# Attention steps dealt out anew in two blocks of a one-core transformer kernel, with pre-scaled queries

## The reference, cut to what matters

```python
s = jnp.einsum('bqhcd,bkhcd->bhcqk', qi, kf) * scale     # scale = 64 ** -0.5
s = jnp.where(kpos[None, :] <= qpos[:, None], s, NEG)
p = jax.nn.softmax(s, axis=-1)
w = p[:, :, 0] - lam * p[:, :, 1]                          # layer A only
```

## Time and profile before

| | us |
|---|---|
| median of three runs (lowest, highest) | 978.34 (976.88, 978.77) |
| the profiled execution | 978.28 |
| its span, first to last instruction | 976.6 |
| TensorE busy, share of the span | 938.0, 96% |
| TensorE's weight loads | 790.2, 81% |
| VectorE busy | 587.7, 60% |
| ScalarE busy | 476.0, 49% |
| GpSimd busy | 70.8, 7% |
| mean granted TensorE clock | 0.990 |

### The profile page before, as it was taken

The page is one execution under the profiler, slowest core; times in us unless marked ns, Lnnn a source line. Parts: engine busy times, 40 slices in busy tenths (PEclk is TensorE's granted clock), DMA queues, the critical chain, the costliest instruction groups (busy, mean ns, idle before and its releaser), DMA issues.

```text
span 976.6 us, 13275 instructions
## 1 busy us (share of the span) xinstructions
PE 938.0 (96%) x4758; PEld 790.2 (81%) x4758; DVE 587.7 (60%) x801; ACT 476.0 (49%) x699; POOL 70.8 (7%) x132
## 2 busy tenths in 40 slices
PE   5999989999999999999999999999897999999998
PEld 4788778888888887778888888888776888888887
DVE  3777766756565576543856555558887374545543
ACT  4765565544444365562744444446335364344341
POOL 2101030100000010001100000002133000000000
PEclk9999999999999999899999999999898999999999
DMA  8844223765655443221765565555332055555551
GB/s 278 298 143 132 87 92 131 258 209 174 201 185 191 154 172 130 87 87 45 258 217 193 176 207 178 167 181 191 113 108 85 3 178 199 182 181 198 179 172 43
DMA packets 95435, 157.77 MB, mean 162 GB/s; under 512 B 5928, under 2 KB 37624, under 8 KB 95392
## 3 DMA queue, kind: packets, MB, share of 16 engines
q1 hardware_dynamic: 93872, 155.09, 47.7%
q10 hardware_dynamic: 1488, 2.10, 0.7%
q0 software_dynamic: 32, 0.02, 0.0%
HBM read 156.12 MB, written 1.06 MB: 161 GB/s over the span
## 4 chain that ended last, share of the span: by engine, by line
PE 85%; DVE 6%; ACT 4%; POOL 2%; issue 2%; DMA 1%; SPq 0%; ACTq 0%; DVEq 0%; POOLq 0%
PE proj L1405 8%; PE proj L1407 8%; PE proj L1406 8%; PE turn L1445 5%; PE score L1405 5%; PE proj L1445 5%; PE score L1406 5%; PE score L1407 5%; PE outp L1405 5%; PE outp L1407 5%; PE outp L1406 5%; PE proj L1449 3%; PE turn L1449 3%; PE turn L1432 2%; PE score L1569 2%
## 5 line engine op out<-in xcount | busy, mean ns | idle before, releaser
L1693 DVE TENSOR_TENSOR wlo<-raw,whi 128x2048 fp32r<-128x2048 f32 x145 | 329.7, 2278 | 221.5 <-ACT whi L1194 147.6
L1194 ACT ACTIVATE whi<-raw 128x2048 fp32r<-128x2048 f32 x64 | 122.6, 1916 | 170.0 <-PE outp L1407 57.5
L1405 PE MATMUL proj<-whi,set 128*128 128x512 f32 (+1 forms) x432 | 174.7, 404 | 9.8 <-DVE wlo L1693 7.0
L1188 ACT ACTIVATE whi<-raw 128x2048 fp32r<-128x2048 f32 (+1 forms) x81 | 153.0, 1901 | 47.6 <-PE outp L1407 18.4
L1407 PE MATMUL proj<-whi,set 128*128 128x512 f32 (+1 forms) x432 | 169.5, 392 | 0.0
L1406 PE MATMUL proj<-wlo,set 128*128 128x512 f32 (+1 forms) x432 | 169.2, 392 | 0.0
L1405 PEld LDWEIGHTS proj<-whi,set 128*128 128x128 f32 x432 | 83.0, 192 | 27.1 <-issue 9.2
L1407 PEld LDWEIGHTS proj<-whi,set 128*128 128x128 f32 x432 | 82.6, 191 | 17.6
L1406 PEld LDWEIGHTS proj<-wlo,set 128*128 128x128 f32 x432 | 83.1, 192 | 15.6
L1405 PE MATMUL score<-whi,set 128*128 128x512 f32 x236 | 92.8, 393 | 0.4 <-ACT e L1331 0.4
L1405 PE MATMUL outp<-whi,set 128*128 128x512 f32 x236 | 92.8, 393 | 0.4 <-issue 0.4
(11 more groups left out here) (207 smaller groups left out, 1240.0 us busy)
## 6 DMA issues: line engine op xcount, KB each, us to landing
raw<-in_a_w_up SPq DMA_DIRECT2D x32, 512.0 KB, 4.3
raw<-in_a_w_down SPq DMA_DIRECT2D x32, 512.0 KB, 4.5
raw<-in_b_w_up SPq DMA_DIRECT2D x32, 512.0 KB, 4.2
raw<-in_b_w_down SPq DMA_DIRECT2D x32, 512.0 KB, 4.4
raw<-in_w_gate SPq DMA_DIRECT2D x22, 512.0 KB, 4.0
raw<-in_w_up SPq DMA_DIRECT2D x22, 512.0 KB, 4.9
raw<-in_w_down SPq DMA_DIRECT2D x22, 512.0 KB, 3.9
raw<-in_a_w_in SPq DMA_DIRECT2D x20, 512.0 KB, 6.6
```

The costliest lines, as they stand in the source:

```text
L1188: act.activation(shaped(whi, u), shaped(raw, u), ACT.Copy).then_inc(hi_done, 1)
L1194: act.activation(shaped(whi, u), shaped(raw, u), ACT.Copy).then_inc(hi_done, 1)
L1405: pe.matmul(out_, hi, wh, start=start, stop=False)
L1693: dve.tensor_tensor(shaped(wlo, u), shaped(raw, u), shaped(whi, u), ALU.subtract).then_inc(lo_done, 1)
```

## The change

- `heads(...)` takes a scale, and ScalarE's copy L1309 applies it, so that the queries in `qk` are already multiplied by 64 ** -0.5. L1869 is gone: the maximum L1868 is written negated, and the exp has no scale. The fill of `flip`, which carried the inverse of the scale to the bias, is 1.
- The step `scores` is split: `scores` keeps TensorE's part, a new step `exps` has the maximum and the exps. By default `exps` follows at once; `diff_pair` writes the scores of both items first and then their `exps`.
- Layer A: the unit order is `qk0`, `v0`, `vm`, ... instead of `qk0`, `vm`, `v0`. The heads of `qk0` are transposed right behind the first half of `v0`, the first diff pair goes before the second half, and all later items, `turn_heads`, `norm`, `rope_chunk` and `split` steps take new places between the product tiles.
- `finish_attention` in layer A has `mix` of the last pair behind `turn_operand`.
- Layer B: the memory and causal items, the `turn_heads`, the evacuation of `kv1` and the `split` steps take new places.

The core of the diff (lines of no consequence left out):

```diff
+        def exps(*items):
+            for it in items:
+                st = add("exps")
+                st.it = it
...
-        mB.append(half_around(lambda: turn_mem("b_mem_norm", 1, 2 * memA[1] + 2), vm, 0, 0, x1[0]))
+        mB.append(half_around(lambda: turn_mem("b_mem_norm", 1, 2 * memA[1] + 2), v0, 0, 0, x1[0]))
+        h_use = [turn_heads(zq[:, 1], [0, 1, 2, 3], qk_pieces(0), rope_ready(r0.rope))[-1]]
+        d = diff_pair(0)
+        exps(*d[0:2])
+        multiply(v0[1], 0, UK, x1[1], "P", False, True, hold=True)
+        mix(d[0]); mix(d[1])
+        ev = evacuate(v0[1], [((0, 512), lambda t: v[:, t, 0:512])], rs_x)
+        split(v0[1] + AHEAD)
+        turn_weights(d[0]); turn_weights(d[1])
+        d += diff_pair(1)
+        exps(*d[2:4])
+        mul_chunk_half(vm, 0, 0, x1, mixed=d[2:4])
+        attend(d[0], vneed); attend(d[1], vneed); turn_weights(d[2]); turn_weights(d[3])
+        norm(d[0:2])
         mul_chunk_half(vm, 1, 0, x1)
...
+        attend(d[2], vneed); attend(d[3], vneed)
+        norm(d[2:4])
+        multiply(qk1[0], 0, 0, x1[0], "P", True, False, hold=True, tiles=[0])
+        qm_use = turn_heads(zq[:, 0], [0, 1], heads(0, 6, 2, SCALE), chunk_ready(ev.chunk))[-1]
+        multiply(qk1[0], 0, 0, x1[0], "P", True, False, hold=True, tiles=[1])
+        split(qk1[0] + AHEAD)
+        m = mem_pair(0)
         mul_chunk_half(qk1, 1, 0, x1, mixed=m[0:2])
         r1 = rope_chunk(qk1[1], 1, rope1, rs_x, zfree[1])
+        turn_weights(m[0]); turn_weights(m[1])
+        m += mem_pair(1)
         mul_chunk_half(qk2, 0, 0, x1, mixed=m[2:4])
...
+        mul_mem(0, 0)
         mul_mem(0, 1)
         mix(d[6]); mix(d[7])
         split(memB[0] + AHEAD)
+        attend(d[4], vneed); attend(d[5], vneed)
         norm(d[4:6])
+        h_use.append(turn_heads(zq[:, 0], [0, 1, 2, 3], qk_pieces(4), rope_ready(r2.rope))[-1])
         mul_mem(1, 0)
+        turn_weights(d[6]); turn_weights(d[7])
+        d += diff_pair(4)
+        exps(*d[8:10])
+        attend(d[6], vneed); o8 = attend(d[7], vneed)
+        norm(d[6:8])
+        mul_mem(1, 1)
         mix(d[8]); mix(d[9])
         split(memB[1] + AHEAD)
+        turn_weights(d[8]); turn_weights(d[9])
+        d += diff_pair(5)
+        exps(*d[10:12])
         ev = evacuate(memB[1], mem_pieces(1), rs_mem, slot_free=zfree[1])
...
             o1 = turn_operand(o_nat, 0, [(None, oset, 0)], (o_evac, o_half), 2 * last_qset_unit + 2)[-1]
+            if items[0].kind == "diff":
+                mix(items[2]); mix(items[3])
             attend(items[0], vneed); attend(items[1], vneed)
...
+        multiply(kv1[1], 0, UK, xk[1], "P", False, True, hold=True, tiles=[1])
         c = [causal_item(0, 0), causal_item(0, 1)]
-        mul_chunk_half(kv1, 1, 0, xk, mixed=(c[0], c[1]))
         ev = evacuate(kv1[1], ...)
...
+        multiply(v1[1], 0, UK, xk[1], "P", False, True, hold=True, tiles=[1])
+        mix(c[4]); mix(c[5])
         ev = evacuate(v1[1], [((0, 512), lambda t: v[:, t, 256:768])], rs_b)
+        split(v1[1] + AHEAD)
         attend(c[2], v_first); attend(c[3], v_first); turn_weights(c[4]); turn_weights(c[5])
...
-                    behind(dve.tensor_reduce(it.nm, S, AX_X, ALU.max))
-                    dve.tensor_scalar(it.nm, it.nm, -SCALE, None, ALU.mult)\
-                       .then_inc(nmax_done, 1)
+                    dve.tensor_reduce(it.nm, S, AX_X, ALU.max, negate=True).then_inc(nmax_done, 1)
```

More of the change, by code:

```diff
@@ L391, in build, with scores @@
         ITEMS = []
-        def scores(kind, pair, t, q, k, need):
+        def scores(kind, pair, t, q, k, need, later=False):
             it = Step()
@@ L409, in scores @@
             st.it = it
-            return it
+            if not later:
+                exps(it)
+            return it
+        def exps(*items):
+            for it in items:
+                st = add("exps")
+                st.it = it
         def mix(it):
@@ L528, in build @@
                       rs_x, slot_free=zfree[0])
-        def mem_item(p, t, qneed, kneed):
-            return scores("mem", p, t, 6 + p, mk[:, p, :], max(qneed, kneed))
-        def diff_item(h, t):
-            return scores("diff", h, t, h, qk[:, 16 + h, :], h_use[h // 2])
-        h_use = [turn_heads(zq[:, 1], [0, 1, 2, 3], qk_pieces(0), rope_ready(r0.rope))[-1]]
-        zfree[1] = h_use[0] + 1
-        multiply(v0[0], 0, 0, x1[0], "P", True, False, hold=True, tiles=[0])
-        d = [diff_item(0, 0), diff_item(0, 1)]
@@ L540, in build @@
-        qm_use = turn_heads(zq[:, 0], [0, 1], heads(0, 6, 2), chunk_ready(ev.chunk))[-1]
-        zfree[0] = qm_use + 1
-        multiply(v0[0], 0, 0, x1[0], "P", True, False, hold=True, tiles=[1])
-        mix(d[0]); mix(d[1])
-        split(v0[0] + AHEAD)
-        turn_weights(d[0]); turn_weights(d[1])
-        d += [diff_item(1, 0), diff_item(1, 1)]
-        multiply(v0[1], 0, UK, x1[1], "P", False, True, hold=True)
-        mix(d[2]); mix(d[3])
-        ev = evacuate(v0[1], [((0, 512), lambda t: v[:, t, 0:512])], rs_x)
@@ L569, in build @@
+        turn_weights(m[2]); turn_weights(m[3])
+        d += diff_pair(2)
+        exps(*d[4:6])
+        multiply(qk2[1], 0, UK, x1[1], "P", False, True, hold=True, tiles=[1])
+        mix(d[4]); mix(d[5])
+        r2 = rope_chunk(qk2[1], 0, rope1, rs_x, zfree[0])
+        split(qk2[1] + AHEAD)
         memB = chunk_units(A["b_w_mem_kv"][0], [(0, 512)])
@@ L572, in mul_mem @@
             multiply(memB[h], 1, UK * h, mB[h], "P", h == 0, h == 1, hold=True, tiles=[t])
+        attend(m[2], memV); attend(m[3], memV)
+        turn_weights(d[4]); turn_weights(d[5])
+        d += diff_pair(3)
+        exps(*d[6:8])
         mul_mem(0, 0)
-        mix(d[4]); mix(d[5])
-        h_use.append(turn_heads(zq[:, 0], [0, 1, 2, 3], qk_pieces(4), rope_ready(r2.rope))[-1])
-        zfree[0] = h_use[2] + 1
-        turn_weights(d[4]); turn_weights(d[5])
-        d += [diff_item(3, 0), diff_item(3, 1)]
         mul_mem(0, 1)
@@ L889, in build @@
         tile(gb, 1, 0, xb)
[L890 removed]
+        qa_use = turn_heads(zq[:, 0], [0, 1, 2, 3], heads(0, 0, 4, SCALE), lambda t: (qn_done, t + 1))[-1]
         zfree[0] = qa_use + 1
@@ L1320, in _ @@
                     act.wait_ge(heads_zeroed, 2)
-                elif st.kind == "scores":
+                elif st.kind == "exps":
                     it = st.it
```

80 lines of the change are left out of this document (40 added, 40 removed).

## The result

The changed kernel takes 992.21 us (median of four runs, 990.99 to 992.61) against 977.61 (976.54 to 978.77) for the kernel before on the same chip: a ratio of 1.0141, 95% interval 1.0129 to 1.0153. The table is of one profiled execution of each.

What follows compares the result with a forecast made beforehand. TensorE, nearly never idle, was taken as the bound, so new waits and clock decide: span 976.6 + 12 (layer A waits) + 6.2 (clock) - 1.7 (layer B) - 0.7 (last layer) = 992.4, plus 1.7: 994.1 us, range 981 to 1001.

Steps and rivals of the forecast that it cites:

- Place A: Layer A, first `turn_heads` and the scores behind it: TensorE waits for T banks and six copies, 3.9 us.
- Place B: Layer A, `qk2[0]`: TensorE waits for bank P from the rope of `qk1[1]`, 1.4 us.
- Place C: Layer A, weights of the fifth pair (d8, d9): mix behind `norm(d[6:8])`, waits 3.4 and 1.2, 4.6 us.
- Place D: Layer A, weights of the last pair: mix behind `turn_operand` and memB's evacuation, waits 5.2 and 1.1, 6.3 us.
- The small ones: Layer A: second item of d6, d7 waits 0.8 for a T bank, two more of 0.15; 1.1 us.
- The clock: Layer A: granted clock falls to half behind A, C and D, costing 2.6, 1.1 and 2.5; +6.2 us.
- GpSimd beside VectorE: Layer A norms: a split's subtraction lengthens GpSimd's first operation; only the norm of d4, d5 meets one, 2 us.
- Layer B: Layer B's stage: waits 6.2 against 6.4, clock 1.8 against 3.3; together -1.7 us, bounds -7 and +3.
- L1869: Removed small operation, 40 times 0.18 us: 0.7 us less in the last layer, elsewhere counted inside the chains.
- The clock stays up: Rival 1: the waits come but the clock does not fall; 991 at most, 986 with the lower bound; chance 0.24.
- Half of it: Rival 2: place C or D is covered, a step put in front being already done; 980 to 984; chance 0.12.
- Faster: the holes of before are what counts: Rival 3: layer B, 379 to 401 us, gives back 4.05 + 3.3, layer A 4.8; 968 or 973; chance 0.08.

Runs made afterwards that it cites:

- fill: Changed kernel plus 13 useless matmuls in layer A, 7 ahead of the first `turn_heads` and 6 between it and the scores: 988.63 us.
- half of v0 ahead: Changed kernel with the first tile of v0's second half moved ahead of the first `turn_heads` in layer A: 986.69 us.
- shift: Changed kernel plus 7 useless matmuls (1.6 us) between the two tiles of v0's second half, so all that follows comes later: 992.49 us.
- mix ahead: Changed kernel with the mix of layer A's last pair (d10, d11) right behind its exps, ahead of memB's evacuation and `turn_operand`: 985.18 us.
- arithmetic alone: Kernel before plus only pre-scaled queries, negated maxima, no L1869, exps without a scale; both layers in the old order: 975.64 us.
- layer B's order: Kernel before plus the new arithmetic and layer B's new order, layer A in the old order: 974.07 us.
- four mends: Changed kernel, layer A: v0 tile ahead of `turn_heads`, norm(d6, d7) behind mix(d8, d9), memB's evacuation and mix(d10, d11) earlier: 982.50 us.
- tiles back: Changed kernel with layer A reordered, a product tile behind the scores of every pair, two at the front and three at the end: 985.17 us.

## Why the prediction was right

The forecast was 994 and the slowdown in layer A; both came. In the span it was +12 of waits and +6.2 of clock in layer A, -1.7 in layer B and -0.7 in the last layer; measured were +8.8, +8.1, -1.0 and -0.8, and -1.1 ahead of the first stage, which belongs to none of its steps. By its steps:

**Place A**, forecast 1.9 + 0.3 + 1.7 = 3.9, measured 1.83 + 0.15 + 1.56 = 3.5: right in each part, and with the releasers named. **Place B**, 1.4 and 1.40.

**Place C**, forecast 3.4 + 1.2, measured 2.99 + 0.70. GpSimd's chain took 2.06 us, from 132.44 to 134.50 (forecast 2.3). The second part was mis-sized: a mix behind another takes 1.2 us, but TensorE is itself busy for 0.5 of them with the first item's weights.

**Place D**, forecast 5.2 + 1.1, measured 3.79 + 0.71: the term furthest off. I counted TensorE's own work between scores and weights as 1.6 us; it took 2.5, from 141.15 to 143.65, as the clock was still down from place C when it began:

```profile
141.15 1.83 PE L1469 MATMUL turn<-ident,o_nat 128*128 128x128 f32 x8
```

At full clock this group takes 1.04 to 1.09. In the three kernels whose slow stretch behind place C was only 3.4 us long (fill, half of v0 ahead, shift) the same wait is 4.53 or 4.54, here in the kernel with the fill:

```profile
144.54 0.33 PE L1633 MATMUL turn<-ident,e 128*128 128x128 f32 x1 [4.53 <-DVE e L1927]
```

So a slow stretch ahead of a wait shortens the wait, and costs less than half of its length. The other 0.5 us is the chain, 6.3 us for 6.8: the split that I put in VectorE's way (0.3) had ended at 139.5, before the scores of d11 had, at 141.4. The experiment with the mix ahead confirms the chain, since with the mix moved bank T was what was late.

**The small ones**, forecast 1.1, measured 0.4. The sum of the waits in layer A was then 13.6 and not 17.3, which is +8.8 over before and not +12.

**The clock**, forecast +6.2 in layer A. All three falls came, and the stage is 16.9 longer where 18.2 were forecast. Of these 16.9, 8.8 are waits; the other 8.1 are busy time of the same matmuls, which is clock. The rows agree nearly: in the three slow stretches TensorE is busy 6.34 + 5.82 + 4.86 = 17.0 us, and half of that is 8.5. So that term was some 2 us short and the waits 3.2 long: two errors of opposite sign, and that the total is nearer than its parts is luck. By falls, half of the busy time is 3.2 for A, 2.9 for C and 2.4 for D, where I had 2.6, 1.1 and 2.5. The mis-sized one is C: I had most of its slow stretch lie in D's wait, but it ended at 142.7 and that wait began at 143.65, so TensorE had work in nearly all of it.

**GpSimd beside VectorE.** The norm of d4, d5 did meet a split: DVE's L1730 and POOL's L1141 in the first two rows of this timeline. The norm of d6, d7 in the last two met none; it is the one that held DVE.

```profile
124.69 2.29 DVE L1730 TENSOR_TENSOR wlo<-raw,whi 128x2048 fp32r<-128x2048 f32 x1 [0.46 <-ACT whi L1225]
...
125.45 1.57 POOL L1141 TENSOR_SCALAR newton<-stat 128x2 f32<-128x2 f32 x1 [42.45 <-ACT junk L1377]
...
132.44 0.19 POOL L1141 TENSOR_SCALAR newton<-stat 128x2 f32<-128x2 f32 x1 [3.54 <-ACT junk L1377]
...
134.53 0.61 DVE L1931 SCALAR_TENSOR_TENSOR o_nat<-outp,stat,subln 128x128 f32<-128x128 f32 x2 [4.06 <-POOL stat L1146]
```

1.57 against 0.19, and the long one ends at 127.02, within 0.04 us of the split's end. The Trainium skill, "SBUF — State Buffer", section "SBUF: two separate sides", says that a VectorE operation with two SBUF inputs and a GpSimd operation that reads SBUF shut each other out for the whole of the one that started first. The trace agrees: the split had started first, and the GpSimd operation ended 0.04 us behind it.

**Layer B**, forecast -1.7 (waits 6.2 for 6.4, clock 1.8 for 3.3), measured -1.0: waits 6.1 for 6.3, and 6.8 us of slow stretch on both sides, in one piece before and in two after. The 2.66 before L1442 was forecast as 2.6. The waits were right in sum, though 0.8 us of what left this stage's old waits came from the arithmetic (6.3 to 5.5) and the order itself added 0.6. The clock's part was a coin: 98.68 or 101.82 us for the same order in two kernels.

**L1869**, forecast -0.7 for the last layer and nothing elsewhere but inside the chains. The last layer gave -0.8 (-0.5 in the kernel with the arithmetic alone, whose medians give -2.4 in all). It was mis-sized in the two attention stages (0.4 and 1.1), where I had it inside the chains and gave it no sum of its own.

**The rivals.** "The clock stays up" is out by the windows. Its 991 has 1.5 us in it that no step gives, and less 4 it is 987, not 986. "Half of it" is out by places C and D. "Faster: the holes of before are what counts" was right in its place and wrong in its size: with the arithmetic, layer B's order and one more step moved, the same stage gives 7.0 us, 4.0 of them clock; it could not cover layer A. The Trainium skill, "VectorE: DVE Perf Modes", section "Rules for kernel authors", advises to minimise the count of operations in a chain. The trace agrees in sign only: of the 8 us that 40 operations of 0.2 us would be, at most 2.4 came.

## What to carry to other kernels

Walk each wait from the end of the last thing that feeds it, step by step through the lists of all engines, and count TensorE's own work in between at the clock that it has there: that gave every wait of the changed kernel to within 1.5 us, its releaser included. It did not carry over to orders with several steps moved at once: four mends had 9.3 us of waits for the expected 4.4, tiles back 12.7 for 2.9. When product tiles are dealt out between attention steps, look at what is left behind the last scores, and at whether a split stands ahead of a mix, an evacuation or a norm on VectorE and ScalarE. Mend one wait at a time and look where it goes: place C's reappeared at D, while the one in layer B, with tiles behind it, was gained in full. That these are the two things that decide is my reading of these orders; the kernel with tiles back shows that the first alone does not.

## What the runs showed of the hardware

- The granted clock falls to half, for 3.4 us, 6.8 and once 10.2, behind some idle stretches of TensorE and not behind others of the same length. At place A it was regular: 6.8 us at half behind holes of 3.5 us in five kernels, 3.4 us behind one of 1.9 us in two, none without a hole in three. In layer B it was not: the same instructions with the same waits had 6.8 us of slow clock in the kernel after, 3.4 in the shifted one and none with the mix ahead. In the table the slow length goes from 10.7 to 44.3 us, worth some 10 us of time by the fitted 0.3.
- It also differs between executions of one kernel: the one with layer B's order took 972.8 us at a mean clock of 0.995 and 977.0 at 0.987, the program being the same. A change that is worth 2 us can be hidden by that, so the waits of one profile tell more than two medians.
- A slow stretch ahead of a wait shortens it: place D's was 3.79 us with 6.8 us at half clock ahead of it and 4.53 with 3.4.
- With the waits of place A filled with useless products the kernel was 3.6 us faster by the medians, and each of its four executions (989.64 at most) was faster than each of the kernel after (990.99 at least).
- A GpSimd operation of 0.19 us took 1.57 beside a VectorE subtraction with both inputs in SBUF, and ended 0.04 us behind it.
